# Convolved projection: high and low activations as one 512-wide matmul into two half banks

## The reference, cut to what matters

```
def conv_ffn(h, w_up, conv_w, conv_b, w_down):
    u = h @ w_up
    up = jnp.pad(u, ((0, 0), (1, 1), (0, 0)))
    u = up[:, :-2] * conv_w[0] + up[:, 1:-1] * conv_w[1] + up[:, 2:] * conv_w[2] + conv_b
    gate, val = jnp.split(u, 2, axis=-1)
    return (jax.nn.silu(gate) * val) @ w_down
```

## Time and profile before

| | |
|---|---|
| time, median of 3 runs | 1955.57 us (1955.13 to 1955.66) |
| span of the profiled execution | 1952.9 us |
| granted TensorE clock | 1.000 |
| TensorE busy | 1924.4 us, 99% |
| VectorE busy | 1325.5 us, 68% |
| ScalarE busy | 1101.8 us, 56% |
| GpSimd busy | 244.2 us, 13% |

### The profile page before, as it was taken

The page is one execution under the profiler, slowest core; times in us unless marked ns, Lnnn a source line. Parts: engine busy times, 40 slices in busy tenths (PEclk is TensorE's granted clock), DMA queues, the critical chain, the costliest instruction groups (busy, mean ns, idle before and its releaser), DMA issues.

```text
span 1952.9 us, 29009 instructions
## 1 busy us (share of the span) xinstructions
PE 1924.4 (99%) x11352; PEld 1658.8 (85%) x11352; DVE 1325.5 (68%) x2282; ACT 1101.8 (56%) x1852; POOL 244.2 (13%) x248
## 2 busy tenths in 40 slices
PE   9999999999999999999999999999999999999999
PEld 8878998887899988888987788888888897778887
DVE  5866976576697657556787875555555688886554
ACT  6666765476676554445567554444444566655442
POOL 1231222033112100000015200000000002310000
PEclk9999999999999999999999999999999999999999
DMA  8434556543455555555543355555555544345553
GB/s 297 143 102 141 192 182 234 180 141 110 140 169 188 200 178 195 186 189 176 173 159 102 108 178 187 187 183 191 181 188 186 183 152 151 98 131 182 188 185 124
DMA packets 90680, 329.83 MB, mean 169 GB/s; under 512 B 10032, under 2 KB 10416, under 8 KB 90288
## 3 DMA queue, kind: packets, MB, share of 16 engines
q1 hardware_dynamic: 90544, 327.98, 51.0%
HBM read 326.89 MB, written 1.05 MB: 168 GB/s over the span
## 4 chain that ended last, share of the span: by engine, by line
PE 88%; DVE 6%; ACT 3%; POOL 1%; issue 1%; DMA 1%; SPq 0%; DVEq 0%; ACTq 0%
PE PS L83 84%; PE PS L86 3%; DVE WL L98 2%; POOL TMP L104 1%; DVE TMP L108 1%; ACT TMP L95 1%; DVE SM L114 1%; ACT WH L92 1%; DMA RAW<-wts 1%; ACT M L92 0%; ACT M L95 0%; SPq L80 0%; ACT TMP L92 0%; DVE SM L108 0%; DVE X L98 0%
## 5 line engine op out<-in xcount | busy, mean ns | idle before, releaser
L98 DVE TENSOR_TENSOR WL<-RAW,WH 128x1024 fp32r<-128x1024 f32 (+1 forms) x609 | 747.2, 1233 | 478.2 <-ACT WH L92 471.9
L92 ACT ACTIVATE WH<-RAW 128x1024 fp32r<-128x1024 f32 (+1 forms) x609 | 641.2, 1057 | 531.8 <-PE PS L83 524.7
L83 PE MATMUL PS<-WH,GH 128*128 128x512 f32 (+1 forms) x1008 | 396.9, 394 | 4.0 <-DVE GL L98 3.9
L83 PE MATMUL PS<-WH,GL 128*128 128x512 f32 (+1 forms) x1008 | 388.2, 385 | 0.0
L83 PE MATMUL PS<-WL,GH 128*128 128x512 f32 (+1 forms) x1008 | 387.8, 385 | 0.0
L83 PE MATMUL PS<-WH,HH 128*128 128x512 f32 (+1 forms) x832 | 315.8, 380 | 0.0
L83 PE MATMUL PS<-WL,HH 128*128 128x512 f32 (+1 forms) x832 | 312.2, 375 | 0.0
L83 PE MATMUL PS<-WH,HL 128*128 128x512 f32 (+1 forms) x832 | 312.2, 375 | 0.0
L83 PE MATMUL PS<-GH,WH 128*128 128x256 f32 x928 | 264.5, 285 | 0.7 <-issue 0.4
L83 PE MATMUL PS<-GL,WH 128*128 128x256 f32 x928 | 262.6, 283 | 0.0
L83 PE MATMUL PS<-GH,WL 128*128 128x256 f32 x928 | 262.6, 283 | 0.0
(11 more groups left out here) (151 smaller groups left out, 2220.1 us busy)
## 6 DMA issues: line engine op xcount, KB each, us to landing
RAW<-wts SPq DMA_DIRECT2D x607, 512.0 KB, 4.0
M<-bias SPq DMA_DIRECT2D x4, 512.0 KB, 11.1
M<-bias SPq DMA_DIRECT2D x1, 2048.0 KB, 9.4
X<-x SPq DMA_DIRECT2D x2, 512.0 KB, 5.4
TMP<-mem SPq DMA_DIRECT2D x1, 1024.0 KB, 11.8
out<-X SPq DMA_DIRECT2D x4, 256.0 KB, 3.8
CST<-cst SPq DMA_DIRECT2D x1, 714.0 KB, 9.5
RAW<-wts SPq DMA_DIRECT2D x2, 256.0 KB, 5.7
```

Source lines behind the costliest of these rows:

```text
L83: return Issued(self.eng and self.eng.matmul(o, l, r, start=first, stop=last, skip_group_check=share))
L92: return Issued(self.eng.activation(o, i, f, scale=scale))
L98: return Issued(self.eng and self.eng.tensor_tensor(o, a, b, op))
```

## The change

`HH` and `HL` become the two halves of one tensor `HX`, `GH` and `GL` those of `GX`, so that high and low activations of one block can be read as one moving operand of 2 x 256 columns. For up tiles 6 to 43 a new function `fm_halves` takes the place of `fm_tile`: `WH` by both at once into the 512 columns of a bank (high part left, low part right), then `WL` by high into the left half. The two halves of the bank then have to be added:
- `rest(n)` on ScalarE copies the right half into the conv buffer `conv_t(n)[:, 1:257]`; it stands last in round n;
- `join(n)` on VectorE adds the left half to it in place; it stands in round n + 1 behind `lows` and ahead of the taps. It signals `made`, which frees the bank;
- `identity(n)` and `taps(n)` read the joined tile in SBUF instead of the bank, and `identity(n)` waits for `join(n)`.

From tile 11 on the taps of tile d come in round d + 2, and both loops get one round more. `product(p)` goes from VectorE to GpSimd, with a signal of its own (`multiplied`); GpSimd's list is now: product one round after the taps, low part three rounds after them.

```
--- before.py
+++ after.py
@@ -146,10 +146,10 @@
             return ctx.enter_context(nc.sbuf_tensor(name, shape, dt))
 
         X = sb("X", [128, 2, 1024])
-        HH = sb("HH", [128, KD, S], FR)
-        HL = sb("HL", [128, KD, S], FR)
-        GH = sb("GH", [128, FF, S], FR)
-        GL = sb("GL", [128, FF, S], FR)
+        HX = sb("HX", [128, 2, KD, S], FR)
+        HH, HL = HX[:, 0, :, :], HX[:, 1, :, :]
+        GX = sb("GX", [128, 2, FF, S], FR)
+        GH, GL = GX[:, 0, :, :], GX[:, 1, :, :]
         RAW = sb("RAW", [128, RAWS, 1024])
         WH = sb("WH", [128, HS, 1024], FR)
         WL = sb("WL", [128, HS, 1024], FR)
@@ -198,6 +198,8 @@
 
         gated = signal("gated")
 
+        multiplied = signal("multiplied")
+
         BANK, HALF = {}, {}
         SIDES = [(HH, HL, 0), (GH, GL, 14)]
         WHOLE = tuple(range(7))
@@ -340,7 +342,7 @@
             return 0 if n <= 2 else 1 if n <= 4 else 2
 
 
-        TAPPED = [6, 6, 7, 7, 8, 9, 9, 10, 11, 11, 12, 12, 13, 14] + [d + 1 for d in range(14, 2 * FF)]
+        TAPPED = [6, 6, 7, 7, 8, 9, 9, 10, 11, 11, 12] + [d + 2 for d in range(11, 2 * FF)]
 
         def taps_at(n):
 
@@ -555,6 +557,25 @@
                         m.then_inc(tile, *done)
                 HALF[key] = h
 
+            def fm_halves(key, acts, xs, allowed=WHOLE):
+
+                ps = take(key, allowed)
+                for i, (ah, _, made_by) in enumerate(acts):
+                    h, o = at[0] // 8, at[0] % 8 * 128
+                    e.wait_ge(lo, h)
+                    e.wait_ge(low_of(made_by), made_by)
+                    wh, wl = WH[:, h % HS, o:o + 128], WL[:, h % HS, o:o + 128]
+                    last = i == len(acts) - 1
+                    e.mm(ps[:, :], wh, xs[:, :, i, :], i == 0, False)
+                    m = e.mm(ps[:, 0:S], wl, ah, False, last)
+                    at[0] += 1
+                    done = [key] if last else []
+                    if at[0] % 8 == 0:
+                        done.append(("half", h))
+                    if done:
+                        m.then_inc(tile, *done)
+                HALF[key] = h
+
             def acts_of(st, side):
                 return [(H(side, k), Lw(side, k), (st, k)) for k in range(KD)]
 
@@ -755,7 +776,7 @@
                 turn_even(("wffn", L), 1, (BANK["rb", ("ffn", L)], BANK["up", L, 0]))
                 fm_tile(("up", L, 5), ffn, (BANK["up", L, 1],))
                 for n in range(6, 2 * FF):
-                    fm_tile(("up", L, n), whole)
+                    fm_halves(("up", L, n), whole, GX[:, :, 14:22, :])
                 acts = [(*G(1, m), ("g", L, m)) for m in range(FF)]
                 run(residual(("down", L), acts, ("mix", 1) if L == 0 else ("f1", 0)))
 
@@ -1298,9 +1319,17 @@
                         e.act(ACT.Identity, conv_c(n), conv_t(n)[:, 1:257], scale=w, bias=col(pb + P_CB + ch)).then_inc(
                             ready, ("id", L, n))
                     else:
-                        e.wait_ge(tile, key)
-                        e.act(ACT.Identity, conv_c(n), bank(key)[:, 0:S], scale=w, bias=col(pb + P_CB + ch)).then_inc(
+                        e.wait_ge(made, key)
+                        e.act(ACT.Identity, conv_c(n), conv_t(n)[:, 1:257], scale=w, bias=col(pb + P_CB + ch)).then_inc(
                             ready, ("id", L, n))
+
+                def rest(n):
+
+                    key = ("up", L, n)
+                    e.wait_ge(tile, key)
+                    if n >= 8:
+                        e.wait_ge(made, ("c", L, n - 8))
+                    e.act(ACT.Copy, conv_t(n)[:, 1:257], bank(key)[:, S:2 * S]).then_inc(aout, ("rest", L, n))
 
                 def gate(p):
                     e.wait_ge(made, ("c", L, 2 * p))
@@ -1308,7 +1337,7 @@
                     e.act(ACT.Silu, c, c).then_inc(ready, ("silu", L, 2 * p))
 
                 def high(p):
-                    e.wait_ge(made, ("gv", L, p))
+                    e.wait_ge(multiplied, ("gv", L, p))
                     e.act(ACT.Copy, G(1, p)[0], conv_c(2 * p + 1)).then_inc(ahi, ("g", L, p))
 
                 highs(("up", L, 0))
@@ -1317,7 +1346,7 @@
                     for t in range(2):
                         e.act(ACT.Copy, even_t(("wffn", L), c, t), X[:, t, c * 512:c * 512 + 512],
                               scale=RX[:, t:t + 1]).then_inc(ready, (("wffn", L), c, t))
-                for n in range(2 * FF + 5):
+                for n in range(2 * FF + 6):
                     if n < 2 * FF:
                         highs(("up", L, n))
                     if n in (1, 3):
@@ -1329,6 +1358,8 @@
                         identity(d)
                     for p in pair_at(n, 0, 1):
                         gate(p)
+                    if 6 <= n < 2 * FF:
+                        rest(n)
                 if L + 1 < DEPTH:
                     run(residual(("down", L), FF, ("mix", L + 1), lambda k: col(pb + P1 + P_MIX + k), 1))
                 else:
@@ -1965,16 +1996,18 @@
                         e.wait_ge(made)
                         e.stt(c, u[:, 2:258], col(w + 88), c, ALU.mult, ALU.add).then_inc(made, ("c", L, n))
                     else:
-                        ps = bank(key)
-                        e.stt(c[:, 1:S], ps[:, 0:S - 1], col(w), c[:, 1:S], ALU.mult, ALU.add).then_inc(made)
+                        u = conv_t(n)
+                        e.stt(c[:, 1:S], u[:, 1:S], col(w), c[:, 1:S], ALU.mult, ALU.add).then_inc(made)
                         e.wait_ge(made)
-                        e.stt(c[:, 0:S - 1], ps[:, 1:S], col(w + 88), c[:, 0:S - 1], ALU.mult, ALU.add).then_inc(
-                            made, ("c", L, n), key)
-                def product(p):
-                    c = conv_t(2 * p + 1)[:, 260:516]
-                    e.wait_ge(ready, ("silu", L, 2 * p))
-                    e.wait_ge(made, ("c", L, 2 * p + 1))
-                    e.tt(c, conv_t(2 * p)[:, 260:516], c, ALU.mult).then_inc(made, ("gv", L, p))
+                        e.stt(c[:, 0:S - 1], u[:, 2:S + 1], col(w + 88), c[:, 0:S - 1], ALU.mult, ALU.add).then_inc(
+                            made, ("c", L, n))
+
+
+                def join(n):
+
+                    key, u = ("up", L, n), conv_t(n)[:, 1:257]
+                    e.wait_ge(aout, ("rest", L, n))
+                    e.tt(u, u, bank(key)[:, 0:S], ALU.add).then_inc(made, key)
 
                 def scaled_tile(n):
 
@@ -1994,10 +2027,10 @@
                     if n in (1, 3):
                         for k in range(2 * n - 2, 2 * n + 2):
                             low_x(("wffn", L), k, gain_f(k), 1)
+                    if 6 <= n - 1 < 2 * FF:
+                        join(n - 1)
                     for d in taps_at(n):
                         taps(d)
-                    for p in pair_at(n, 1, 1):
-                        product(p)
                 if L + 1 < DEPTH:
                     run(residual(("down", L), FF, ("mix", L + 1), lambda k: col(pb + P1 + P_MIX + k), 1))
                 else:
@@ -2391,10 +2424,17 @@
                 for n in range(6):
                     m = e.fill(conv_t(n)[:, 0:258:257], 0.0)
                 m.then_inc(edged, L)
-                for p in range(FF):
-                    gh, gl = G(1, p)
-                    e.wait_ge(ahi, ("g", L, p))
-                    e.tt(gl, conv_t(2 * p + 1)[:, 260:516], gh.bitcast(F32), ALU.subtract).then_inc(glo, ("g", L, p))
+                for n in range(2 * FF + 6):
+                    for p in pair_at(n, 1, 1):
+                        c = conv_t(2 * p + 1)[:, 260:516]
+                        e.wait_ge(ready, ("silu", L, 2 * p))
+                        e.wait_ge(made, ("c", L, 2 * p + 1))
+                        e.tt(c, conv_t(2 * p)[:, 260:516], c, ALU.mult).then_inc(multiplied, ("gv", L, p))
+                    for p in pair_at(n, 1, 3):
+                        gh, gl = G(1, p)
+                        e.wait_ge(ahi, ("g", L, p))
+                        e.tt(gl, conv_t(2 * p + 1)[:, 260:516], gh.bitcast(F32), ALU.subtract).then_inc(
+                            glo, ("g", L, p))
             for L in range(DEPTH):
                 e.wait_ge(small, ("scl", L, 0))
                 for b in (1, 2):
```

## The result

| | before | after |
|---|---|---|
| time, median of 5 runs | 1955.57 us (1955.13 to 1955.78) | 2018.06 us (2017.63 to 2018.85) |
| ratio to before | | 1.0321 (95%: 1.0310 to 1.0331) |
| span of the profiled execution | 1952.9 us | 2015.8 us |
| that execution's own time | not listed | 2017.63 us |

A forecast was written before the change was run, and what follows sets the result against it. TensorE bound the kernel before; afterwards ScalarE and VectorE waiting on each other would. Loss of 25.4 us per layer, 50.8 for two, plus the 1952.9 span and 2.7 to the median gives 2006.4, stated as 2006; range 1992 to 2028.

The forecast's parts named there:

- The ring: Up stage: ScalarE and VectorE wait on each other once per tile, 3.43 us even rounds, 3.74 odd, where TensorE needs 2.77.
- the port: VectorE and GpSimd steps on SBUF exclude each other; 0.17 us for each of 16 pairs, 2.7 us.
- Loads: Up stage work per pair of tiles: VectorE 5.0 us, ScalarE 4.05 us, both fitting in 5.55 us.
- the first rival: Up stage: mutual waiting does not bind, TensorE keeps the pace at 2.77 us per round; 1947.5 us, chance 0.06.
- so round 11 starts at 214.4: Up stage, first layer: start of round 11 on ScalarE, after round 10's subtraction, join, identity, gate and rest.
- From there down runs at its 2.72 us a half as before: Down projection from its fourth weight half, starting at 341.5: unchanged pace, nothing given back.
- TensorE's own half before is long done: Start of down: TensorE finishes its preceding half long before the fourth half starts at 341.5.
- a rest of 0.36 and an identity of 0.58 per round: Upper bound for ScalarE's two steps without overlap with the next: 12 us more, 2018.
- TensorE's saving: Up tiles 6 to 43: a 512-wide matmul replaces two narrow ones, 0.013 us a step, 608 steps, 8.1 us.
- The pace of 0.346 us a step: Sign expected in the profile after: TensorE's time per 128-row step of the up stage between stalls.

## Why the prediction was right, point by point

**The ring** was forecast at 3.43 and 3.74 us plus 0.17 a pair for the port, 7.34 in all; measured 7.38. By pieces: weight copy to subtraction 1.08 and 1.09 (1.08), subtraction to join 1.27 and 1.14 (1.14, and the 0.13 is the port), join to identity 0.44 and 0.51 (0.45), identity 0.51 (0.49), rest 0.26 (0.27), gate 0.31 (0.31). The two runs with an extra step, and the runs that cut the ring in two different ways (join first; identity and taps a round later), show that it was the cause.

**Loads** are what the first rival went by. It was wrong for the changed kernel, and half right behind it: with join moved alone, VectorE's load and port losses, 5.74 us a pair, were the next limit.

**Where 12 us were missed.** 50.8 us were forecast against 62.9 us of span, 25.4 against some 31.3 a layer. In the first layer:
- "so round 11 starts at 214.4": it started at 216.34, 1.9 late. Some 1.3 us of that is the port, whose term was only taken from round 11 on: beside GpSimd the taps of rounds 7 and 8 took 2.16 and 1.51 us instead of 1.91 and 1.00, and the weight subtraction of round 10 took 1.76 instead of 1.22. The rest is a backlog of VectorE. The forecast let its subtraction of round 9 wait for ScalarE's copy and start at 208.4; in the trace VectorE is busy without a gap before it, and it starts at 209.85. Without the port losses it would have started at about 209.1, still 0.7 late.
- 32 rounds from there to the weight copy at 334.55: 118.2 against 117.4, 0.8 more.
- from that copy to the fourth half of down: 10.3 us (to 344.89) against 9.6, 0.7 more. Half of it is the last four tap steps, which took 2.27 us beside GpSimd instead of 1.90.
- "From there down runs at its 2.72 us a half as before": wrong. The half took 5.14 us (344.89 to 350.03) and in the second layer 4.7 (731.34 to 736.04) because of the clock, 2.4 and 2.0 us. The prediction had an idle time of TensorE in its own numbers ("TensorE's own half before is long done") and did not ask what the clock would do. The run that fills the gap gives 4.4 us for both layers.

Together 5.8 us; 31.15 - 25.4 = 5.75 us were missed in this layer. VectorE in rounds 7 to 10 of the changed kernel (taps of rounds 7 and 8, subtractions of rounds 9 and 10), and its last taps:

```profile
204.87 2.16 DVE L108 SCALAR_TENSOR_TENSOR TMP<-TMP,PAR 128x256 f32<-128x256 f32 x4
...
208.41 1.51 DVE L108 SCALAR_TENSOR_TENSOR TMP<-TMP,PAR 128x256 f32<-128x256 f32 x2
209.85 1.21 DVE L98 TENSOR_TENSOR WL<-RAW,WH 128x1024 fp32r<-128x1024 f32 x1
...
213.14 1.76 DVE L98 TENSOR_TENSOR WL<-RAW,WH 128x1024 fp32r<-128x1024 f32 x1
...
338.84 2.27 DVE L108 SCALAR_TENSOR_TENSOR TMP<-TMP,PAR 128x255 f32<-128x255 f32 x4
```

The measured time falls in the stated range, and one of its bounds is even the same number: "a rest of 0.36 and an identity of 0.58 per round" were to give 2018. That is luck. The two steps cost 0.26 and 0.51 us, as forecast, and the missing 12 us came from the four places above.

**TensorE's saving** of 8.1 us was never visible under the ring. By itself it was 4.6 us in the order of the diff. The pace of 0.346 us a step that was to show between stalls was wrong: wide and narrow in turn take 0.353.

**GpSimd and the port**: 0.12 us a pair instead of 0.17; its direct share is the 4 us that went with the product's return.

## What to carry to other kernels

When two in-order queues hand each other work, follow the hand-overs once around before adding up loads: here both engines had about 1 us idle or more in every round (0.97 to 1.75) and still set the pace, because a step on ScalarE waited for something that stood on VectorE behind the answer to ScalarE's own last step. One round more of delay between producer and reader cuts such a ring at next to no cost (2013.8 to 1952.1 us). A queue that is only just faster than the bound does not catch up on its backlog within a stage, so look at what is late at its end, and at what TensorE's clock does after the stall.

## What the runs showed of the hardware

- **Half clock after a stall.** Where TensorE had been idle for 5.0, 4.6 and 3.45 us, a spell at half clock followed: at once in the first two, and in the last (join first, product on VectorE) only after a full-speed restart at 317.42, as the last fence shows: in its two stretches the granted clock, the third number from the end, is 0.76 and 0.77. The short idle times of the ring, up to 1 us each, left it at 1.00 (258 to 340 us of the changed kernel). Filled with other matmuls, the longest gap left it at 1.00 too.
- **The port.** Where GpSimd's 0.74 us step met a VectorE step with two SBUF inputs, it cost VectorE between 0.12 us (the ring's weight subtraction) and 0.54 us (that of round 10), and GpSimd up to 1 us. An addition of PSUM and SBUF did not lengthen: join took 0.41 us at 214.82 of the changed kernel, in the middle of a GpSimd step (213.78 to 215.50).
- **Wide beside narrow.** 512 and 256 columns in strict alternation take 0.353 us a pair of matmuls, in twos 0.348, in eights 0.349.

```profile
317.40:320.40 3.00, 2.98 (x10) 2.42 (x11) 3.00 (x3) 1.46 (x2) 3.00 (x4) 0.76 0.58 179
321.00:324.00 3.00, 3.00 (x12) 2.39 (x11) 1.45 (x2) 1.06 (x1) 0.74 (x2) 0.77 0.87 279
```
